# Gate and up of two pairs of steps by seven block products for eight, in four feed-forward stages

## The chip, the cores and the metric

One core of a Trainium2 chip runs the whole program. The metric is the device time in microseconds of one execution. The engines are named TensorE (PE in the profile), VectorE (DVE), ScalarE (ACT), GpSimd (POOL) and SyncE (SP, which issues the loads of the weights).

## The reference

256 tokens of width 1024, in float32, go through a first block (pool mixer, mLSTM, attention, and a feed-forward part with a short convolution) and then through a second block of two layers. Each of these has a feed-forward part, a mixer (NSA attention in the first layer, HGRN2 in the second) and another feed-forward part:

```python
def _swiglu(x, w_gate, w_up, w_down):
    return (jax.nn.silu(x @ w_gate) * (x @ w_up)) @ w_down
x = _layer_norm(alpha * x + 0.5 * _swiglu(x, ffn1_w_gate[i], ffn1_w_up[i], ffn1_w_down[i]), ...)
```

`w_gate` and `w_up` are 1024 x 2816, `w_down` is 2816 x 1024. These four feed-forward parts are what the change is about.

## The kernel before

The plan (from line 438) lists eleven stages: 0, 4 and 8 are linear projections into the mixers, 1, 5 and 9 projections out of them, 2 is the feed-forward part with a convolution, and 3, 6, 7 and 10 are the four plain feed-forward stages.

**Precision.** Every product is made of three matmuls with float32r operands. An operand is split into a high part (ScalarE copies it, which rounds: `act_split` and `act_split_next`, lines 552 and 570) and a low part (VectorE subtracts the high part, `dve_split` and `dve_split_next`, lines 562 and 578). `token_pass` (lines 751 to 753) issues high x high, low x high, high x low, with 128 tokens as the stationary operand and 512 columns of weights moving.

**A step of a feed-forward stage** covers 256 of the 2816 inner columns; there are 11 (`FFN_STEPS`, 0 to 10). For each of the two token tiles `gate_up` (line 911) forms gate and up together, 2 x 256 columns in one PSUM bank: first with the upper 512 rows of the weights (kh = 0, called k0 below), then the lower 512 (k1), 12 matmuls each; 48 a step. ScalarE takes silu of the gate half (line 1003), VectorE multiplies by the up half (line 1055). In the next step TensorE turns the product (four transposes, line 927, into bank 3), ScalarE and VectorE split it into `ghi` (line 1008) and `glo` (line 1060), and `pe_down_step` (line 907) adds its product with two blocks of 128 rows of `w_down` to banks 4 to 7: 24 matmuls. So TensorE's order in a step (`step`, line 934) is k0 of both tiles, the transposes of the step before, k1 of both tiles, the down matmuls of the step before.

**Buffers and queues.** Weights come in halves of 128 x 1024 floats, 512 KB: four of gate and up (two k0, two k1) and two of down a step. SyncE loads them in this order into a ring of six raw slots, each when the low part of the half six places before is made. The split halves go to a ring of six slots (`whi`, `wlo`); ScalarE may overwrite one when TensorE has counted it off in `half_done`. Every engine works through its own order written out by hand (`pe_ffn`, `act_ffn`, `dve_ffn`): for ScalarE ghi, k0 of the next step, silu, silu, k1 and down of the next step; for VectorE glo, the low parts of k0, two products, the low parts of k1 and down. The steps between the first two and the last are a hardware loop (`Fori`) on each of the four engines.

**Around it.** The stage's activations `ahi`, `alo` are made at its opening (`pe_turn`, `act_turned` line 736, `dve_turned` line 741); GpSimd makes a small power for the norms (`pool_rstd`, line 719), loads gain and bias (`pool_load_gb`, lines 633 and 634), and loads the first weights of the NSA stage (`pool_load_nsa`, line 2274) early, while the convolution stage runs. The arena, a large buffer, holds the data of the mixers and lies mostly unused in the feed-forward stages.

Of the kernel before, what the change touches and what calls it, by code (L numbers as in the profile page):

```python
# [63 lines left out]
EXTRA_SLOTS = 2  # L64

# [60 lines left out]
def build_program(nc, io, const_at, out):  # L126
    ctx = ExitStack()
    with ctx:
# [218 lines left out]

        KC_AT = (32, 160, 224, 352)
# [60 lines left out]
        stored = sem("stored")  # L409
        dve_chain = sem("dve_chain")  # L410
# [46 lines left out]
        w_halves, slab0, half0 = [], [0], [0]  # L457

        def add_half(slab, mode, part, extra=None):
            ring = sum(x[3] < HALF_SLOTS for x in w_halves)  # L460
            w_halves.append((slab, mode, part, ring % HALF_SLOTS if extra is None else HALF_SLOTS + extra))

        PROJ_ORDER = {1: (0, 1), 5: (0, 1), 9: (0, 1)}
        for n, e in enumerate(plan):
# [18 lines left out]
            else:  # L483
                for j in range(FFN_STEPS):
                    g = b + (3 * j - 1 if j else 0)
                    for i in range(4):
                        m, x = divmod(i, 2) if e[0] == "conv" and j else (i % 2, i // 2)
                        add_half(g + m, "part", x)
# [17 lines left out]
        for h, (_, mode, part, _) in enumerate(w_halves):  # L506
            if mode != "part" and part == 1:
                landed.append(landed[-1])
                continue
            landings[h % RAW_SLOTS] += 1  # L510
            landed.append((h % RAW_SLOTS, landings[h % RAW_SLOTS]))

        def raw_pair(h):

            at = h % RAW_SLOTS
            return raw[:, at:at + 2, :].rearrange("p s (k n) -> p (s k) n", k=4)

        def raw_half(h):
# [6 lines left out]
            return raw[:, h % RAW_SLOTS, :]  # L525
# [29 lines left out]
        def dve_split(dve, h):  # L555
# [6 lines left out]
            dve.tensor_tensor(lo, raw_half(h), hi.bitcast(F32), ALU.subtract).then_inc(lo_ready, 1)  # L562

# [169 lines left out]

        def act_turned(act, p, a, h):
# [152 lines left out]
        def silu_count(n):  # L887

            return FFN_STEPS + 2 * FFN_STEPS * ffn_index(n)
# [27 lines left out]
        def pe_ffn(pe, n, p):  # L917
            f = ffn_index(n)
            mults, turns = 2 * FFN_STEPS * f, (FFN_STEPS + 1) * f

            def gate_up(h, a, kh):
                return pe_pair(pe, h + 2 * kh, kh, a, ps[:, a, :], kh == 0, kh == 1)

            def turn(tiles):
                for x in range(2):
                    for a in tiles:
                        last = pe.transpose(ps[:, 3, x * T + a * P:x * T + (a + 1) * P],  # L927
                                            gated[:, a, x * P:(x + 1) * P], ident)
                last.then_inc(g_turned, 1)

            for a in range(NT):
                pe_normed(pe, p, half0[n], a, ps[:, a, :], gu_done)

            def step(j, by_mults, by_halves):
                h = body(n, 1)
# [2324 lines left out]
```

## Time and profile before

| | us |
|---|---|
| median of three runs | 1361.31 |
| lowest and highest of them | 1361.13, 1361.77 |
| span of the profiled execution, first to last instruction | 1361.0 |
| TensorE busy | 1349.7 |
| VectorE busy | 883.2 |
| ScalarE busy | 682.4 |
| GpSimd busy | 123.1 |

The profiled execution has its span alone, no device time of its own; the span is 0.3 us below the median of the runs. A feed-forward step lasts 16.8 us, the four stages hold 44 of them, so these are over half of the time. The line numbers of the rows are those of the kernel before. A TensorE row shows an instruction's own duration, which overlaps with the next; how far apart two of them start is read from their start times.

### The profile page before, as it was taken

The numbers are of one execution on the slowest core, as the hardware profiler recorded it, in microseconds if no ns is written. First come the engines' busy times: TensorE is split into PE (matmuls) and PEld (weight loads), VectorE is DVE, ScalarE is ACT, GpSimd is POOL, SyncE is SP. The second block draws the span as 40 slices with busy tenths as digits, with TensorE's granted clock in tenths as the row PEclk, the third lists the DMA queues.
The fourth block names the chain that finished last, engine by engine and source line by source line (L and its number), as shares of the span: only waits on it lengthen the run. The fifth ranks groups of instructions, "written<-read, shape, count | busy, mean of one in ns | idle before, by whom it ended". The sixth has DMA issues, their size and how long they took to land.

```text
span 1361.0 us, 21006 instructions
## 1 busy us (share of the span) xinstructions
PE 1349.7 (99%) x7477; PEld 1158.8 (85%) x7477; DVE 883.2 (65%) x1280; ACT 682.4 (50%) x1037; POOL 123.1 (9%) x235
## 2 busy tenths in 40 slices
PE   9999999999999999999999999999999999999997
PEld 6988999998888889988888888888889988888886
DVE  5877876676555584688655558555576988755555
ACT  6673655554444435595444444444446854444441
POOL 5431000000000011282000000000000001000000
PEclk9999999999999999999999999999999999999999
DMA  9435865564555547504655554655555434655550
GB/s 317 155 99 179 294 196 184 187 191 156 189 189 189 190 136 226 177 2 154 229 189 186 185 195 154 239 185 185 185 159 189 163 108 156 204 190 190 188 186 31
DMA packets 189944, 241.64 MB, mean 178 GB/s; under 512 B 7809, under 2 KB 171922, under 8 KB 189890
## 3 DMA queue, kind: packets, MB, share of 16 engines
q1 hardware_dynamic: 184304, 226.52, 50.9%
q0 software_dynamic: 5296, 13.29, 3.1%
q10 hardware_dynamic: 290, 1.11, 0.2%
q8 instruction: 35, 0.57, 0.2%
q14 instruction: 19, 0.16, 0.0%
HBM read 238.24 MB, written 1.07 MB: 176 GB/s over the span
## 4 chain that ended last, share of the span: by engine, by line
PE 98%; DVE 1%; POOL 1%; DMA 0%; ACT 0%; issue 0%; DVEq 0%; POOLq 0%
PE ps L751 20%; PE ps L753 20%; PE ps L752 20%; PE ps L583 6%; PE ps L585 6%; PE ps L584 6%; PE ps L774 2%; PE ps L775 2%; PE ps L781 2%; PE ps L927 1%; PE ps L1466 1%; PE ps L2756 1%; PE ps L902 1%; PE ps L1477 1%; PE ps L727 1%; PE ps L2338 1%
## 5 line engine op out<-in xcount | busy, mean ns | idle before, releaser
L578 DVE TENSOR_TENSOR wlo<-raw,whi 128x1024 fp32r<-128x1024 f32 x270 | 323.2, 1223 | 121.3 <-ACT whi L570 118.0
L570 ACT ACTIVATE whi<-raw 128x1024 fp32r<-128x1024 f32 x270 | 277.3, 1056 | 117.6 <-PE ps L753 95.2
L751 PE MATMUL ps<-whi,ahi 128*128 128x512 f32 x776 | 308.2, 397 | 0.0
L753 PE MATMUL ps<-wlo,ahi 128*128 128x512 f32 x776 | 302.7, 390 | 0.0
L752 PE MATMUL ps<-whi,alo 128*128 128x512 f32 x776 | 302.4, 390 | 0.0
L562 DVE TENSOR_TENSOR wlo<-raw,whi 128x1024 fp32r<-128x1024 f32 x142 | 168.8, 1221 | 35.4 <-ACT whi L552 35.1
L583 PE MATMUL ps<-ahi,whi 128*128 128x256 f32 x624 | 177.9, 285 | 0.0
L585 PE MATMUL ps<-ahi,wlo 128*128 128x256 f32 x624 | 177.3, 284 | 0.0
L584 PE MATMUL ps<-alo,whi 128*128 128x256 f32 x624 | 177.2, 284 | 0.0
L753 PEld LDWEIGHTS ps<-wlo,ahi 128*128 128x128 f32 x776 | 145.7, 188 | 31.5
L751 PEld LDWEIGHTS ps<-whi,ahi 128*128 128x128 f32 x776 | 145.9, 188 | 30.0 <-issue 0.9
L752 PEld LDWEIGHTS ps<-whi,alo 128*128 128x128 f32 x776 | 146.0, 188 | 29.0 <-issue 0.2
L552 ACT ACTIVATE whi<-raw 128x1024 fp32r<-128x1024 f32 x142 | 144.4, 1054 | 37.6 <-PE ps L753 23.4
L751 PE MATMUL ps<-whi,ghi 128*128 128x512 f32 x400 | 156.5, 391 | 0.0
L752 PE MATMUL ps<-whi,glo 128*128 128x512 f32 x400 | 155.8, 389 | 0.0
L753 PE MATMUL ps<-wlo,ghi 128*128 128x512 f32 x400 | 155.7, 389 | 0.0
L583 PEld LDWEIGHTS ps<-ahi,whi 128*128 128x128 f32 x624 | 120.3, 193 | 0.9 <-issue 0.3
L1060 DVE TENSOR_TENSOR glo<-ps,ghi 128x512 fp32r<-128x512 f32 x40 | 27.7, 692 | 143.8 <-ACT ghi L1008 143.8
L584 PEld LDWEIGHTS ps<-alo,whi 128*128 128x128 f32 x624 | 120.4, 193 | 0.5
L585 PEld LDWEIGHTS ps<-ahi,wlo 128*128 128x128 f32 x624 | 120.4, 193 | 0.0
L1008 ACT ACTIVATE ghi<-ps 128x512 fp32r<-128x512 f32 x40 | 24.0, 600 | 172.6 <-PE ps L927 172.6
L719 POOL TENSOR_TENSOR rstd<-spread_sq,consts 128x1 f32<-128x1 f32 x16 | 12.9, 808 | 975.2 <-DVE spread_sq L686 973.6
(438 smaller groups left out, 1806.5 us busy)
## 6 DMA issues: line engine op xcount, KB each, us to landing
raw<-ffn_w_gate SPq DMA_DIRECT2D x88, 512.0 KB, 3.7
raw<-ffn_w_up SPq DMA_DIRECT2D x88, 512.0 KB, 4.7
raw<-ffn_w_down SPq DMA_DIRECT2D x88, 512.0 KB, 4.3
raw<-w_up SPq DMA_DIRECT2D x44, 512.0 KB, 4.4
raw<-w_down SPq DMA_DIRECT2D x22, 512.0 KB, 4.2
raw<-w_in SPq DMA_DIRECT2D x16, 512.0 KB, 5.3
raw<-nsa_w_in SPq DMA_DIRECT2D x8, 1024.0 KB, 5.1
raw<-hgrn_w_in SPq DMA_DIRECT2D x16, 512.0 KB, 4.7
```

Source lines behind the costliest of these rows:

```text
L552: act.activation(split_half(w_slots(slot)[0], mode), raw_half(h), ACT.Copy).then_inc(hi_ready, 1)
L562: dve.tensor_tensor(lo, raw_half(h), hi.bitcast(F32), ALU.subtract).then_inc(lo_ready, 1)
L570: act.activation(split_half(w_slots(slot)[0], mode), raw_half(h), ACT.Copy).then_inc(hi_ready, 1)
L578: dve.tensor_tensor(lo, raw_half(h), hi.bitcast(F32), ALU.subtract).then_inc(lo_ready, 1)
L583: pe.matmul(dst, wh, ah, start=first, stop=False, skip_group_check=True)
L584: pe.matmul(dst, wh, al, start=False, stop=False, skip_group_check=True)
L585: return pe.matmul(dst, wl, ah, start=False, stop=last, skip_group_check=True)
L751: pe.matmul(dst, a_h, w_h, start=first, stop=False, skip_group_check=True)
L752: pe.matmul(dst, a_l, w_h, start=False, stop=False, skip_group_check=True)
L753: return pe.matmul(dst, a_h, w_l, start=False, stop=last, skip_group_check=True)
L774: pe.matmul(dst, a_h, wh[:, :, k, :], start=first and k == 0, stop=False, skip_group_check=True)
L1060: dve.tensor_tensor(lo[:, :, cols], ps[:, 3, :].rearrange("p (x t) -> p x t", x=2)[:, :, cols], hi[:, :, cols].bitcast(F32), ALU.subtract) ...
```

## The change

In stages 3, 6, 7 and 10 the steps 3 and 4, and the steps 6 and 7, are made as a pair. The pair's gate columns (2 x 256) and up columns are the two block columns, the weights' upper and lower 512 rows the two block rows: blocks b11 (gate, upper), b12 (up, upper), b21, b22 of 512 x 512. With the two token tiles and the two halves of the depth this is a 2 x 2 by 2 x 2 product of blocks, and it is made by seven products of 12 matmuls: b21, b11, b22 with plain or summed activations, t1 to t4 being differences of blocks: t1 = b12 - b11, t2 = b22 - t1, t3 = b22 - b12, t4 = b21 - t2.

- The four raw blocks of a pair, 1 MB each, are loaded whole into the arena (`load_block`), those of the first pair behind the down rows of step 1, those of the second in the single step behind the first pair (step 5), and don't pass through the raw ring. `b1_landed` counts r11 and r12.
- VectorE makes the differences (`dve_t`) in the arena, t1 and t2 for the first pair at the end of step 1, for the second pair in step 5 (t1 ahead of its first `glo`), t3 and t4 in the step ahead of the pair.
- Blocks are split 128 x 2048 at a time into two neighbouring slots of the ring of six (`act_block`, `dve_block`), which so holds three blocks. In the order of a stage, `c` counts blocks; for a pair it is b21, b11, t1, t2, down of the step before, t3, b22, t4, then k0 and k1 of the next step and the pair's two down blocks.
- GpSimd makes the sums of activation blocks at a stage's opening (`pool_sums`); ScalarE and VectorE split them once a stage in step 1 (`s_hi`, `s_lo`, in the arena).
- The products are accumulated in banks z, 1 and r, with copies of two partial sums and additions (`v1`, `v5`, `v_u2`, in `xc`); gate and up then have 512 columns each for a tile.
- Tile 0 of the single steps alternates between banks 0 and 2.
- The hardware loops of the four stages are gone, all steps are written out on every engine.
- The loads of the first NSA weights wait for the last pair of stage 3, the load of `r_gain` for that of stage 7. In the NSA and HGRN stages some semaphores are merged, with the order of the work as it was.

The core of the diff (PE, then ACT, then DVE, POOL and SP; functions that build names and counts are left out):

```diff
+DOUBLES = {3: (3, 6), 6: (3, 6), 7: (3, 6), 10: (3, 6)}
+SUM_BUFFERS = {"b21": "r21", "b11": "r11", "t1": "n1", "t2": "n2", "t3": "r12", "b22": "r22", "t4": "r21"}
...
+        _, s_hi = split_view(0, "s_hi", 4, 4, P)
+        _, s_lo = split_view(2048, "s_lo", 4, 4, P)
...
+        x11, x12, x21, x22 = (blocks["n1"][:, i, :] for i in range(4))
+        s_sum = blocks["n2"]
+        xc_flat = xc.rearrange("p a b -> p (a b)")
+        v1, v_u2, v5, g1 = (xc_flat[:, 512 * i:512 * i + 512] for i in range(4))
...
+        def act_block(act, n, c):
+            name, h = order[n][c]
...
+            if name[0] == "t":
+                act.wait_ge(t_ready, 4 * g.d + int(name[1]))
+            else:
+                landed_at, each = block_landed["r" + name[1:]]
+                act.wait_ge(landed_at, each * (g.d + 1))
+            act.wait_ge(half_done, before_in_slot[h + 1] + 1)
+            act.activation(hi, src, ACT.Copy).then_inc(hi_ready, 2)
+        def dve_block(dve, n, c):
...
+            dve.wait_ge(hi_ready, h + 2)
+            dve.tensor_tensor(lo, src, hi.bitcast(F32), ALU.subtract).then_inc(lo_ready, 2)
...
+        def dve_t(dve, g, i):
...
+            if i == 1:
+                dve.wait_ge(b1_landed, 32 * (g.d + 1))
+                dst, a, b = n1, r12, r11
+            elif i == 2:
+                dve.wait_ge(b22_landed, 16 * (g.d + 1))
+                dve.wait_ge(t_ready, 4 * g.d + 1)
+                dst, a, b = n2, r22, n1
+            elif i == 3:
+                dst, a, b = r12, r22, r12
+            else:
+                dve.wait_ge(b21_landed, 16 * (g.d + 1))
+                dve.wait_ge(t_ready, 4 * g.d + 2)
+                dst, a, b = r21, r21, n2
+            dve.tensor_tensor(dst, a, b, ALU.subtract).then_inc(t_ready, 1)
...
+        def pool_sums(pool, p):
...
+            wait_activations(pool, p)
+            for dst, a, kh in ((x11, 0, 0), (x12, 0, 1), (x21, 1, 0), (x22, 1, 1)):
+                hi, lo = (turned_tile(v, a, kh).bitcast(F32) for v in (ahi, alo))
+                last = pool.tensor_tensor(dst.rearrange("p (c n) -> p c n", c=4), hi, lo, ALU.add)
+            chain(last)
+            pool.tensor_tensor(s_sum[:, 2, :], x11, x21, ALU.subtract)
+            chain(pool.tensor_tensor(s_sum[:, 0, :], x21, x22, ALU.add))
+            chain(pool.tensor_tensor(s_sum[:, 1, :], s_sum[:, 0, :], x11, ALU.subtract))
+            pool.tensor_tensor(s_sum[:, 3, :], x12, s_sum[:, 1, :], ALU.subtract).then_inc(sums_ready, 1)
...
+            def single(i):
+                g, k0, k1 = parts[i], parts[i].at["k0"], parts[i].at["k1"]
+                done = mults + 2 * (i - 1)
+                pe.wait_ge(lo_ready, k0 + 2)
+                if g.first == parts[i - 1].first:
+                    pe.wait_ge(gated_ready, done + 1)
+                gate_up(k0, 0, 0, g.first)
+                pe.wait_ge(gated_ready, done + (1 if parts[i - 1].double else 2))
+                gate_up(k0, 1, 0, 1).then_inc(half_done, 2)
+                pe.wait_ge(gated_ready, done + 2)
+                if parts[i - 1].double:
+                    turn(pair_step(0), range(NT))
+                else:
+                    turn(own, range(NT))
+                pe.wait_ge(lo_ready, k1 + 2)
+                gate_up(k1, 0, 1, g.first).then_inc(gu_done, 1)
+                if parts[i - 1].double:
+                    pe.wait_ge(g_ready, turns + parts[i - 1].steps[0] + 1)
+                    turn(pair_step(1), range(NT))
+                gate_up(k1, 1, 1, 1).then_inc(half_done, 2)
+                for j, source in zip(parts[i - 1].steps, ((ghi, glo), (last_ghi, last_glo))):
+                    down_step(g, j, source)
+            def double(i):
+                g = parts[i]
+                d, z, r, done = g.d, g.first, 2 - g.first, mults + 2 * (i - 1)
+                def product(name, act_k, bank, first, last):
...
+                    pe.wait_ge(lo_ready, h + 2)
+                    for k in range(4):
+                        ins = token_pass(pe, ps[:, bank, :], act_k(k), (wh[:, k, :], wl[:, k, :]), first and k == 0, last and k == 3)
+                    ins.then_inc(half_done, 2)
...
+                pe.wait_ge(gated_ready, done + 1)
+                product("b21", block(0, 1), r, True, True)
+                product("b11", block(0, 0), z, True, True)
+                pe.wait_ge(gated_ready, done + 2)
+                pe.wait_ge(s_lo_ready, f + 1)
+                product("t1", block_sum(1), 1, True, True)
+                turn(own, range(NT))
+                pe.wait_ge(snap_ready, 3 * d + 1)
+                product("t2", block_sum(2), z, False, True)
+                down_step(g, parts[i - 1].steps[0], (ghi, glo))
+                pe.wait_ge(snap_ready, 3 * d + 3)
+                product("t3", block_sum(3), z, False, True)
+                product("b22", block_sum(4), 1, False, True)
+                pe.wait_ge(c_ready, 2 * d + 2)
+                product("t4", block(1, 1), z, False, True)
...
+            def single(i):
+                g, c = parts[i], place_of(n, parts[i].at["k0"])
+                before = parts[i - 1]
+                turned((0, 1), turns + before.steps[0] + 1)
+                act_block(act, n, c + 3)
+                if i == 1:
+                    act.wait_ge(sums_ready, f + 1)
+                    act.wait_ge(half_done, half0[n])
+                    act.activation(s_hi.rearrange("p a k n -> p (a k n)"), s_sum.rearrange("p a n -> p (a n)"),
+                                   ACT.Copy).then_inc(s_hi_ready, 1)
+                if before.double:
+                    turned((0, 1), turns + before.steps[1] + 1, last_ghi)
+                for a in range(NT):
+                    silu(i, a)
+                act_block(act, n, c + 4)
+                act_block(act, n, c + 5)
+                if before.double:
+                    act_block(act, n, c + 6)
+            def double(i):
+                g, c = parts[i], place_of(n, parts[i].at["b21"])
+                d, z = g.d, ps[:, g.first, :]
+                act_block(act, n, c + 3)
+                act.wait_ge(half_done, g.at["b11"] + 2)
+                act.activation(v1, z, ACT.Copy).then_inc(snap_ready, 1)
+                act_block(act, n, c + 4)
+                act.wait_ge(half_done, g.at["t1"] + 2)
+                act.activation(v5, ps[:, 1, :], ACT.Copy).then_inc(snap_ready, 1)
+                turned((0, 1), turns + parts[i - 1].steps[0] + 1)
+                act_block(act, n, c + 5)
+                act.wait_ge(half_done, g.at["t2"] + 2)
+                act.activation(v_u2, z, ACT.Copy).then_inc(snap_ready, 1)
+                act.wait_ge(c_ready, 2 * d + 1)
+                act.activation(v1, v1, ACT.Silu).then_inc(silu_ready, 1)
+                act_block(act, n, c + 6)
+                act_block(act, n, c + 7)
+                act_block(act, n, c + 8)
+                act_block(act, n, c + 9)
+                act.wait_ge(half_done, g.at["t4"] + 2)
+                act.activation(g1, z, ACT.Silu).then_inc(silu_ready, 1)
+                act_block(act, n, c + 10)
...
+            def single(i):
+                g, c = parts[i], place_of(n, parts[i].at["k0"])
+                before, following = parts[i - 1], parts[i + 1]
+                late = following.double and (before.double or i == 1)
+                if late:
+                    dve_t(dve, following, 1)
+                turned((0, 1), turns + before.steps[0] + 1)
+                dve_block(dve, n, c + 3)
+                if before.double:
+                    turned((0, 1), turns + before.steps[1] + 1, last_ghi, last_glo)
+                    c += 1
+                product(i, 0)
+                if late:
+                    dve_t(dve, following, 2)
+                product(i, 1)
+                if i == 1:
+                    dve.wait_ge(s_hi_ready, f + 1)
+                    dve.tensor_tensor(s_lo.rearrange("p a k n -> p (a k n)"), s_sum.rearrange("p a n -> p (a n)"),
+                                      s_hi.rearrange("p a k n -> p (a k n)").bitcast(F32), ALU.subtract).then_inc(s_lo_ready, 1)
+                if before.double:
+                    dve_block(dve, n, c + 3)
+                if following.double:
+                    dve_t(dve, following, 3)
+                dve_block(dve, n, c + 4)
+                if following.double:
+                    dve_t(dve, following, 4)
+                dve_block(dve, n, c + 5)
+                if not following.double and i + 2 < final and parts[i + 2].double:
+                    dve_t(dve, parts[i + 2], 1)
+                    dve_t(dve, parts[i + 2], 2)
+            def double(i):
+                g, c = parts[i], place_of(n, parts[i].at["b21"])
+                d, z, r = g.d, ps[:, g.first, :], ps[:, 2 - g.first, :]
+                dve_block(dve, n, c + 3)
+                dve.wait_ge(snap_ready, 3 * d + 1)
+                dve.tensor_tensor(v1, r, v1, ALU.add).then_inc(c_ready, 1)
+                dve_block(dve, n, c + 4)
+                turned((0, 1), turns + parts[i - 1].steps[0] + 1)
+                dve_block(dve, n, c + 5)
+                dve_block(dve, n, c + 6)
+                dve_block(dve, n, c + 7)
+                dve.wait_ge(half_done, g.at["t3"] + 2)
+                dve.wait_ge(snap_ready, 3 * d + 3)
+                dve.tensor_tensor(v5, z, v5, ALU.add).then_inc(c_ready, 1)
+                dve_block(dve, n, c + 8)
+                dve.wait_ge(half_done, g.at["b22"] + 2)
+                link(dve, dve_chain, "dve", dve.tensor_tensor(v_u2, ps[:, 1, :], v_u2, ALU.add))
+                dve.wait_ge(silu_ready, silus + 2 * i + 1)
+                dve.tensor_tensor(v1, v1, v_u2, ALU.mult).then_inc(gated_ready, 1)
+                dve_block(dve, n, c + 9)
+                dve.wait_ge(silu_ready, silus + 2 * i + 2)
+                dve.wait_ge(c_ready, 2 * d + 2)
+                dve.tensor_tensor(g1, g1, v5, ALU.mult).then_inc(gated_ready, 1)
+                dve_block(dve, n, c + 10)
...
-            pool.wait_ge(a_ready, tile_half(1, 1, 1))
+            pool.wait_ge(half_done, last_double(3).at["t4"] + 2)
...
+            def block_free(n, g, name):
+                before = doubles[g.d - 1] if g.d else None
+                if before is not None and (before in groups[n] or n == 7):
+                    reader = {"r11": "t1", "r12": "t3", "r22": "b22", "r21": "t4"}[name]
+                    sp.wait_ge(lo_ready, before.at[reader] + 2)
+                else:
+                    sp.wait_ge(half_done, half0[2 if n == 3 else n])
+            def load_block(n, g, name, mats):
...
+                block_free(n, g, name)
+                sp.dma_start(blocks[name], mats[int(name[2]) - 1][row:row + 512, col:col + 512]
+                             .rearrange("(k p) n -> p k n", p=P)).then_inc(block_landed[name][0], 16)
+            def load_ffn(n, mats):
...
+                    if not g.double:
...
+                    after_double = len(g.downs) == 2
+                    if after_double and following is not None:
+                        load_block(n, following, "r11", mats)
+                    for x, (j, h) in enumerate(g.downs.items()):
...
+                        if after_double and x == 0 and following is not None:
+                            for name in ("r12", "r22", "r21"):
+                                load_block(n, following, name, mats)
+                    if i == 1 and following is not None:
+                        for name in ("r11", "r12", "r22", "r21"):
+                            load_block(n, following, name, mats)
...
-                if p == 5:
+                if p > 4:
+                    pool_sums(pool, p - 1)
+                if p == 6:
+                    pool.wait_ge(half_done, last_double(7).at["t4"] + 2)
                     pool.dma_start(r_gain, io["hgrn_norm_gain_2"].rearrange("a d -> d a")).then_inc(r_gain_landed, 16)
```

## Rows read from the trace of the kernel before

**Rows 1.** The page: busy time and share of the span; the chain that ended last.
```profile
PE 1349.7 (99%) x7477; PEld 1158.8 (85%) x7477; DVE 883.2 (65%) x1280; ACT 682.4 (50%) x1037; POOL 123.1 (9%) x235
...
PE 98%; DVE 1%; POOL 1%; DMA 0%; ACT 0%; issue 0%; DVEq 0%; POOLq 0%
```

**Rows 2.** The page's costliest groups: name, count, busy us, mean ns, idle before.
```profile
L751 PE MATMUL ps<-whi,ahi 128*128 128x512 f32 x776 | 308.2, 397 | 0.0
L753 PE MATMUL ps<-wlo,ahi 128*128 128x512 f32 x776 | 302.7, 390 | 0.0
```

**Rows 3.** Stretches: length, then PE, PEld, DVE, ACT, POOL busy (instructions), clock, DMA share, GB/s.
```profile
376.00:392.80 16.80, 16.80 (x78) 13.89 (x77) 8.61 (x10) 7.29 (x9) 0.00 (x0) 1.00 0.58 185
...
660.00:677.00 17.00, 17.00 (x78) 14.06 (x78) 12.49 (x13) 9.89 (x12) 0.00 (x0) 1.00 0.88 291
...
309.00:317.00 8.00, 8.00 (x44) 6.71 (x44) 3.83 (x7) 4.27 (x7) 0.00 (x0) 1.00 0.11 40
```

**Rows 4.** Timeline, TensorE, around one step of stage 3: start us, duration us, instruction.
```profile
374.49 0.39 PE L751 MATMUL ps<-whi,ahi 128*128 128x512 f32 x1
...
383.14 0.39 PE L751 MATMUL ps<-whi,ahi 128*128 128x512 f32 x1
...
391.30 0.39 PE L751 MATMUL ps<-whi,ahi 128*128 128x512 f32 x1
...
394.02 0.39 PE L751 MATMUL ps<-whi,ahi 128*128 128x512 f32 x1
```

**Rows 5.** Timeline of the same step, ScalarE and VectorE, idle time before in brackets.
```profile
380.57 0.60 ACT L1008 ACTIVATE ghi<-ps 128x512 fp32r<-128x512 f32 x1 [4.82 <-PE ps L927]
381.06 2.00 ACT L570 ACTIVATE whi<-raw 128x1024 fp32r<-128x1024 f32 x2
381.20 0.69 DVE L1060 TENSOR_TENSOR glo<-ps,ghi 128x512 fp32r<-128x512 f32 x1 [4.19 <-ACT ghi L1008]
382.15 2.36 DVE L578 TENSOR_TENSOR wlo<-raw,whi 128x1024 fp32r<-128x1024 f32 x2 [0.26 <-ACT whi L570]
383.34 0.38 ACT L1003 ACTIVATE ffn_buf<-ps 128x256 f32<-128x256 f32 x1 [0.28 <-PE ps L753]
```

**Rows 6.** Groups by line and shape, VectorE and ScalarE: the widths that the change uses.
```profile
L2961 DVE TENSOR_TENSOR arena<-arena 128x2048 f32<-128x2048 f32 x1 | 2.3, 2292 | 0.0
...
L741 DVE TENSOR_TENSOR alo<-ps,ahi 128x512 fp32r<-128x512 f32 x32 | 21.6, 687 | 12.7 <-ACT ahi L736 12.7
...
L2843 ACT ACTIVATE arena<-arena 128x2048 f32<-128x2048 f32 x1 | 1.9, 1920 | 0.0
...
L1191 ACT ACTIVATE ffn_buf<-ffn_buf 128x512 f32<-128x512 f32 x11 | 7.0, 633 | 26.7 <-DVE ffn_buf L1259 26.7
```

**Rows 7.** Timeline, stage 0: GpSimd's widest operations and VectorE's beside them.
```profile
46.38 2.41 DVE L562 TENSOR_TENSOR wlo<-raw,whi 128x1024 fp32r<-128x1024 f32 x2
47.57 2.16 POOL L2197 TENSOR_TENSOR sq<-sq 128x542 f32<-128x542 f32 x1
...
49.82 1.15 POOL L2198 TENSOR_TENSOR sq<-sq 128x538 f32<-128x538 f32 x1
...
55.73 1.29 POOL L2207 TENSOR_TENSOR xc<-xc,sq 128x512 f32<-128x512 f32 x1
```

**Rows 8.** Timeline, the opening of stage 6 and its step 1.
```profile
646.56 0.69 DVE L660 SCALAR_TENSOR_TENSOR xc<-ps,x_tok 128x512 f32<-128x512 f32 x1
...
654.12 2.35 DVE L562 TENSOR_TENSOR wlo<-raw,whi 128x1024 fp32r<-128x1024 f32 x2
...
655.07 0.53 POOL L634 DMA_DIRECT2D sq<-ln_bias  x1
...
656.39 0.41 DVE L1055 TENSOR_TENSOR ffn_buf<-ffn_buf,ps 128x256 f32<-128x256 f32 x1
...
659.79 4.63 DVE L562 TENSOR_TENSOR wlo<-raw,whi 128x1024 fp32r<-128x1024 f32 x4 [0.53 <-ACT whi L552]
...
664.31 0.60 ACT L1008 ACTIVATE ghi<-ps 128x512 fp32r<-128x512 f32 x1 [1.70 <-PE ps L927]
```

**Rows 9.** The page's DMA issues: KB each, median us from issue to landing.
```profile
raw<-nsa_w_in SPq DMA_DIRECT2D x8, 1024.0 KB, 5.1
...
arena<-nsa_cmp_w POOLq DMA_DIRECT2D x2, 1024.0 KB, 10.9
```

More of the change, by code:

```diff
@@ L885, in ffn_index, with mult_count, single_count @@
             return (3, 6, 7, 10).index(n)
-        def silu_count(n):
-            return FFN_STEPS + 2 * FFN_STEPS * ffn_index(n)
+        def mult_count(n):
+            return 2 * sum(len(groups[m]) for m in groups if m < n)
+        def single_count(n):
+            return sum(not g.double for m in groups if m < n for g in groups[m])
         def pe_down(pe, h, x, a, n, first=False, last=False, gated_parts=(ghi, glo)):
@@ L917, in pe_ffn, with gate_up @@
         def pe_ffn(pe, n, p):
[L918 to L924, printed above, removed]
+            f, parts = ffn_index(n), groups[n]
+            mults, turns = mult_count(n), (FFN_STEPS + 1) * f
+            final = len(parts) - 1
+            def gate_up(h, a, kh, bank):
+                return pe_pair(pe, h, kh, a, ps[:, bank, :], kh == 0, kh == 1)
@@ new lines, in pair_step, with down_step @@
+            def pair_step(i):
+                return lambda a, x: (v1, g1)[a][:, i * 256 + x * P:i * 256 + (x + 1) * P]
+            def down_step(g, j, source):
+                h = g.downs[j]
+                pe.wait_ge(g_ready, turns + j + 1)
+                for x in range(2):
+                    pe.wait_ge(lo_ready, h + x + 1)
+                    for a in range(NT):
+                        for m in range(2):
+                            last = pe_down(pe, h + x, x, a, m, j == 0 and x == 0, gated_parts=source)
+                    last.then_inc(half_done, 1)
@@ L1027, in act_ffn @@
+            act_table(act, ACT.Silu)
+            silu(0, 0)
+            silu(0, 1)
+            act_block(act, n, 3)
+            act_block(act, n, 4)
+            for i in range(1, final):
+                if parts[i].double:
+                    double(i)
+                else:
+                    single(i)
             b = half0[n + 1]
+            act.wait_ge(half_done, last_double(n).at["b22"] + 2)
             act_split(act, b - 2)
@@ L1075, in dve_ffn @@
+            product(0, 0)
+            product(0, 1)
+            dve_block(dve, n, 3)
+            dve_block(dve, n, 4)
+            for i in range(1, final):
+                if parts[i].double:
+                    double(i)
+                else:
+                    single(i)
             b = half0[n + 1]
```

351 lines of the change are left out of this document (214 added, 137 removed).

## The prediction

> **What bounds the kernel now.** I read four views in this order. First the page's busy shares and its chain that ended last [rows 1]: TensorE is busy for 1349.7 of 1361.0 us and holds 98% of the chain, while VectorE is busy 65% and ScalarE 50%. Second the costliest groups [rows 2]: the 128x512 matmuls of lines 751 to 753 are the largest part, and all three have 0.0 idle before them. Third the stretches of one step of a feed-forward stage [rows 3]: 16.80 us, TensorE busy throughout, VectorE 8.6, ScalarE 7.3, at a granted clock of 1.00 (the upper level, 2.4 GHz). Fourth the timeline of such a step [rows 4, 5]. So time is gained only by issuing less on TensorE, and it is lost only where a helper engine is late for it. The question is whether twice the helper work in a pair of steps still hides.
>
> **The price of a matmul.** A row's 390 ns is not it, since matmuls overlap. In [rows 4] twelve of them (line 751 at 391.30, again at 394.02) are 2.72 us apart, 0.227 us each; a step is 72 of them and four transposes, 374.49 to 391.30 = 16.81 us, of which the transposes take 0.45. By a rule of the Trainium skill (TensorE: Matmul & The Clock Gate, Back-to-back issue gap) load-and-multiply pairs of 512 columns sustain about 131 ns; the trace disagrees with its 227. By that figure the saving below would be 12.6 us; the measurement decides.
>
> **What is removed.** A pair of steps needs gate and up of 2 token tiles x 2 halves of the depth: 8 block products of 4 x 3 = 12 matmuls, 96. The scheme has 7, 84. The 48 matmuls of the two down steps and the eight transposes stay. Saved: 12 x 0.227 = 2.72 us a pair, with two pairs in each of four stages 8 x 2.72 = **21.8 us**. Written-out code in place of hardware loops: at a loop's end the trace shows no gap (the period 16.81 spans it), and straight-line stretches show TensorE just as full (the third of [rows 3]); zero either way.
>
> **What is added.** Per pair: VectorE makes 7 low halves of 128x2048 for 8 of 128x1024, four differences t1 to t4, three PSUM additions. [Rows 6] price them: 2.29 us for 2048 columns on VectorE, 1.92 on ScalarE, 0.69 and 0.60 to 0.63 for 512. VectorE goes from 2 x 8.6 = 17.2 to 7 x 2.29 + 4 x 2.29 + 4 x 1.18 + 3 x 0.69 + 2 x 0.69 + 2 x 0.69 = 34.7 us, against 30.9 us of TensorE in the pair; only because the differences are put into the single steps around does it fit. ScalarE: 7 x 1.92 + 4 x 1.0 + 3 x 0.60 + 2 x 0.63 + 2 x 0.60 = 21.7 us. So I laid out a timetable of the double step from these durations and the handoffs of [rows 4, 5]: ScalarE starts 0.20 us after a product's last slot (383.34 against 383.14), VectorE 0.03 us after ScalarE. D = 0 is the first matmul of b21.
> TensorE, if never held: b21 to 2.72, b11 5.44, t1 8.16, transposes 8.61, t2 11.33, down 16.77, t3 19.49, b22 22.21, t4 24.93.
> ScalarE (the ring holds three blocks, so a block's split waits for the product three before): t2 2.9 to 4.8, v1 copy 6.2, down 8.2, v5 copy 9.0, ghi 9.6, t3 11.5, v_u2 copy 12.1, silu 12.8, b22 14.7, t4 17.0 to 18.9 (it waits for the down step's second half), next k0 19.7 to 21.7, next k1 24.4, silu 25.8, down 27.8.
> VectorE: t2 4.9 to 7.2, v1 7.9, down 10.2, glo 10.9, t3 13.8, b22 17.0, t4 18.9 to 21.2, v5 21.9, k0 24.3, v_u2 25.0, product 25.7, k1 28.1, product 28.8, down 31.1.
> Ready against wanted: t2 7.2 / 8.6; glo 10.9 / 11.3; t3 13.8 / 16.8; b22 17.0 / 19.5; t4 with v5 21.9 / 22.2; next k0 24.3 / 24.9; the pair's second product 28.8 / 30.4. Nothing is late, but two margins are 0.3 to 0.4 us: if the cover goes, t4 is late next, and what queues behind it on VectorE is k0. Bounds for what these margins leak: nothing, or (each of the two 0.3 us over its margin) 0.6 us a pair, 5 us in all. I take zero, as every duration in them is a row.
>
> The single step between the two pairs (step 5) is another matter. Its VectorE order is the rest of the pair (free at 31.1 - 24.9 = 6.2 in its own time), then t1 (8.5), then glo (9.2). TensorE wants glo before it may overwrite bank 3 with the second set of transposes, at 5.44 + 0.45 + 2.72 = 8.6. It waits **0.6 us**, once a stage: 2.4 us. Bounds: 0, and 2.3 (the whole of t1) a stage, 9 us; I take the timetable's. Behind t1 on VectorE are glo, the split of the second down step and the products; with them 3 us late nothing of TensorE's is reached. Steps 2 and 8, the other neighbours of a pair, have glo before the differences or none to make, and wait for nothing.
>
> GpSimd makes the sums of the activations, eight operations of 128x512 at 1.15 to 1.29 us [rows 7], 10 us, behind two gain and bias transfers that it issues. In stage 6 these end at 655.6 and ScalarE comes to its wait for the sums at about 667 (ghi at 664.31, 0.6, a pair of splits 2.0) [rows 8]. 655.6 + 10 = 666: just in time. ScalarE late by x delays silu, k1 and the down split; VectorE then has the sums' low half (2.29), t1 and t2 (4.5) ahead of the next glo, which the timetable has ready at 7.9 of the next step against 11.3 wanted. So the first 3 us of lateness cost nothing. Stage 3 has 5 us more, having issued its transfers before.
>
> Transfers: bytes are the same, but four blocks of 1 MB now go ahead of the k0 of step 2. In stage 6 they wait for the projection's last product (read by line 660 at 646.56, [rows 8]); at the 291 GB/s that the queues reached in 660 to 677 [rows 3] 4.2 MB take 14 us, to 661, and k0's 1 MB 3.6 us, to 664.6, where ScalarE asks for it at 664.9. Hidden, barely; lateness would add to the sums' below (A). In stage 3 the queue is idle then (share 0.11 in 309 to 317 [rows 3]). One 1 MB transfer lands in 5.1 us [rows 9]. In the second pair r12, r22, r21 go out as t3, b22, t4 are split (13.8, 17.0, 21.2), and the down rows behind them at 24.3, landing by about 30; ScalarE asks for those at 24.9 + 6.7 = 31.6. The NSA stage's first weights (10.9 us to land, [rows 9]) move from the convolution stage to the end of stage 3's second pair, some 50 us ahead of that stage. GpSimd holds its two memsets and the rstd behind that wait; nothing asks for them earlier. The NSA and HGRN edits rename semaphores: zero. r_gain moves from stage 6 to the last pair of stage 7, still a stage before its reader, and the rstd queued behind its wait is asked for only at that stage's end: zero.
>
> **Sum.** 21.8 - 2.4 = 19.4 us off. The profiled execution spans 1361.0, 0.3 below the median of 1361.3: 1361.3 - 19.4 = **1341.9 us**.
>
> **Rivals.**
> A, the sums are locked out, and thin margins leak (chance 0.20): [rows 7] show a GpSimd operation of 542 columns that starts at 47.57 under two VectorE splits (46.38 to 48.79) and takes 2.16, and its sister of 538 columns, beside operations with other inputs, 1.15. With every one of the eight held for a split of 1.2, the sums end near 675, 8 us late; but VectorE only has six splits there [rows 8], so 5 us is the most: 667 becomes 672. Past the free 3 us it costs TensorE 1 to 2 us in each of stages 6, 7, 10: 3 to 6 us, and up to 5 from the margins. 1345 to 1351. Against: VectorE is idle or reads PSUM from 656.5 to 659.8. The Trainium skill (SBUF — State Buffer, two separate sides) says the pair of ports is an exclusive lock between GpSimd and a VectorE operation with two SBUF inputs; by that rule, the trace agrees, A's lower part is due.
> B, most of the gain is given back (0.05): the handoffs in a pair are slower than in the quiet steps (91% of VectorE's pair is busy: 22.7 of 24.9), t4 and k0 slip 0.7 to 1 us each: 1.4 to 2 us a pair, 11 to 16 us; 1353 to 1358.
> C, the other side (0.05): the split chain paces the pair. From a slot freed to a low half ready is 0.2 + 1.92 + 0.03 + 2.29 = 4.4 us; two products cover 5.4. If, through VectorE's queue order (additions waiting ahead of a split), only one product covers it, TensorE waits 4.4 - 2.7 = 1.7 us at t2, b22, t4 and k0: 6.8 a pair, 54 us, less 21.8: slower by 30 us, 1394. It decides from 2.7 us of waiting a pair. For: VectorE's order in the pair is fixed by hand. Against: the timetable puts every addition at a point where its input is there.
> The rest (0.02) is no change. That the change computes eight products anyway is excluded by its code: seven calls of 12.
>
> **How the numbers follow.** My case has 0.68: from 1339.5 (no wait at all) to 1345. The range must reach into A: 1339 to 1350 holds 0.68 + most of 0.20. From this kernel about 0.2% (2.7 us) can be told from no change. Faster by more: 0.68 + 0.20 + 0.05 less a little = 0.92; within: 0.03; slower: 0.05.
>
> **What the profile should show.** Products of 12 matmuls 2.72 us apart inside a pair; 24.9 us from b21 to the next k0; matmuls fewer by 96; VectorE busy up by 8 x 17.5 = 140 us, ScalarE by 8 x 7 = 56 (and by 9 and 8 for the sums); a wait of TensorE on VectorE's glo of about 0.6 us once a stage, in step 5; none on the splits. The prediction is wrong if TensorE waits on low halves inside the pairs (B, C), or if ScalarE waits long for GpSimd's sums in step 1 and glo of step 2 is late (A).

## The result and the profile after

| | before | changed |
|---|---|---|
| median of 16 runs each, us | 1362.62 | 1359.30 |
| lowest and highest, us | 1361.13, 1365.15 | 1356.80, 1364.24 |
| span of the profiled execution, us | 1361.0 | 1356.6 |

The ratio is 0.9977, with a 95% interval of 0.997 to 0.9985: 3.3 us faster, where 19.4 were forecast. The time lies outside the range given.

The changed kernel's page: busy time and share, then two of the costliest groups (as in [rows 1, 2]). The last line is from the page of the kernel before.
```profile
PE 1335.0 (98%) x7380; PEld 1144.7 (84%) x7381; DVE 1050.8 (77%) x1316; ACT 738.8 (54%) x1041; POOL 178.8 (13%) x267
...
L640 DVE TENSOR_TENSOR wlo<-raw,whi 128x1024 fp32r<-128x1024 f32 x294 | 380.8, 1328 | 65.5 <-ACT whi L630 63.6
...
L899 PE MATMUL ps<-whi,ahi 128*128 128x512 f32 x616 | 248.1, 403 | 10.1 <-DVE wlo L640 10.1
...
L578 DVE TENSOR_TENSOR wlo<-raw,whi 128x1024 fp32r<-128x1024 f32 x270 | 323.2, 1223 | 121.3 <-ACT whi L570 118.0
```
The reader should see three things. TensorE has 97 matmul records fewer (the code issues 96 fewer) and 14.7 us less busy time. VectorE's mean low half of 128x1024 takes 1328 ns where it took 1223. And the matmuls of line 899 have 10.1 us of idle time before them, released by those low halves; before, that column held 0.0.

Where a matmul stood in both traces tells where the time went. The same matmuls are taken in each stage: the first of the opening's high pass, the first with `last_ghi` at the end.

| us between them | before | changed | difference |
|---|---|---|---|
| stage 3, opening to end | 174.85 | 169.43 | -5.42 |
| end of 3 to end of 6 | 334.19 | 334.04 | -0.15 |
| end of 6 to end of 7 | 186.93 | 186.83 | -0.10 |
| end of 7 to end of 10 | 333.18 | 334.17 | +0.99 |

Stage 3 gains all of its 5.44 us. Stages 6 and 7 each lose about as much again as their pairs save, stage 10 a microsecond more. The waits of TensorE, longest first, in the changed kernel (engine, line, for whom: us in total, times, longest) say how:
```profile
PE ps L899 <- DVE wlo L640: 10.1, 3, 3.4
PE ps L1644 <- DVE zeros L1732: 1.2, 1, 1.2
```
The first line is three waits, one in each of those stages. This is the timeline of stage 6's opening there:
```profile
648.98 7.57 DVE L640 TENSOR_TENSOR wlo<-raw,whi 128x1024 fp32r<-128x1024 f32 x2
649.36 0.57 POOL L766 DMA_DIRECT2D sq<-ln_gain  x1 [5.03 <-DVE alo L889]
...
650.48 4.99 POOL L875 TENSOR_TENSOR arena<-ahi,alo 128x512 f32<-128x512 f32 x4
...
655.54 2.16 POOL L877 TENSOR_TENSOR arena<-arena 128x512 f32<-128x512 f32 x1
...
657.14 8.33 DVE L640 TENSOR_TENSOR wlo<-raw,whi 128x1024 fp32r<-128x1024 f32 x4
```
Two low halves, the k0 of step 1, that took 2.35 us at this place before [rows 8] take 7.57: they are not through until GpSimd's four additions (650.48 to 655.47) are. The first half takes its usual 1.22 us, and this is the second alone:
```profile
650.11 6.44 DVE L640 TENSOR_TENSOR wlo<-raw,whi 128x1024 fp32r<-128x1024 f32 x1
```
TensorE wanted it at 653.2. Its own timeline at that point:
```profile
652.18 1.07 PE L929 MATMUL ps<-whi,alo 128*128 128x512 f32 x4
656.61 0.68 PE L899 MATMUL ps<-whi,ahi 128*128 128x512 f32 x1 [3.36 <-DVE wlo L640]
657.08 0.63 PE L900 MATMUL ps<-whi,alo 128*128 128x512 f32 x1
...
659.64 0.63 PE L900 MATMUL ps<-whi,alo 128*128 128x512 f32 x1
660.07 0.45 PE L901 MATMUL ps<-wlo,ahi 128*128 128x512 f32 x1
660.36 0.40 PE L899 MATMUL ps<-whi,ahi 128*128 128x512 f32 x1
```
After an idle time of 3.36 us the matmuls are 0.43 us apart and not 0.227, eight of them here, some 13 in stage 10. Stretches over both places (columns as in [rows 3]) show the granted clock:
```profile
649.00:657.00 8.00, 4.64 (x20) 3.57 (x19) 8.00 (x5) 4.83 (x8) 7.54 (x7) 0.99 1.04 403
657.00:661.00 4.00, 4.00 (x12) 3.13 (x11) 4.00 (x4) 0.45 (x1) 3.92 (x3) 0.60 0.85 254
1177.00:1181.00 4.00, 4.00 (x11) 3.14 (x10) 4.00 (x4) 0.26 (x1) 3.92 (x3) 0.50 0.95 301
```
0.50 is the lower level of 1.2 GHz; the stretch with 0.60 holds its end. So a stage pays 3.5 us for the wait and its edge, and then for the clock: in stage 6 the nine spacings from 656.61 to 660.36 take 3.75 us where nine of 0.227 take 2.04, 1.7 us more; in stage 10, counted in the same way, it is 2.9 us.

**Theories.** L: GpSimd's sums shut VectorE out of its low halves, and that is the whole loss; the pairs give what their matmuls say. L1 adds that the port is held across the four additions because GpSimd waits nowhere between them. W: something else eats the gain, the written-out code or the pairs.

### The profile page after: what moved, and what is told of

It reads as the page before. It is cut to its first block, busy times and chain, and to the rows that moved or that the text cites. A ratio compares the mean times of both kernels' runs of the same rounds, so it can differ in the third digit from the quotient of the medians.

```text
span 1356.6 us, 19292 instructions
## 1 busy us (share of the span) xinstructions
PE 1335.0 (98%) x7380; PEld 1144.7 (84%) x7381; DVE 1050.8 (77%) x1316; ACT 738.8 (54%) x1041; POOL 178.8 (13%) x267
## 4 chain that ended last, share of the span: by engine, by line
PE 96%; DVE 3%; DMA 0%; ACT 0%; POOL 0%; issue 0%; SPq 0%; DVEq 0%
PE ps L899 20%; PE ps L900 20%; PE ps L901 20%; PE ps L716 6%; PE ps L718 6%; PE ps L717 6%; PE ps L922 2%; PE ps L929 2%; PE ps L923 2%; DVE wlo L640 2%; PE ps L1080 1%; PE ps L1775 1%; PE ps L3059 1%; PE ps L1054 1%; PE ps L1786 1%; PE ps L860 1%
## 5 line engine op out<-in xcount | busy, mean ns | idle before, releaser
L640 DVE TENSOR_TENSOR wlo<-raw,whi 128x1024 fp32r<-128x1024 f32 x294 | 380.8, 1328 | 65.5 <-ACT whi L630 63.6
L630 ACT ACTIVATE whi<-raw 128x1024 fp32r<-128x1024 f32 x294 | 298.5, 1053 | 88.5 <-PE ps L901 72.9
L899 PE MATMUL ps<-whi,ahi 128*128 128x512 f32 x616 | 248.1, 403 | 10.1 <-DVE wlo L640 10.1
L900 PE MATMUL ps<-whi,alo 128*128 128x512 f32 x616 | 242.9, 394 | 0.0
L901 PE MATMUL ps<-wlo,ahi 128*128 128x512 f32 x616 | 242.5, 394 | 0.0
L677 DVE TENSOR_TENSOR wlo<-arena,whi 128x2048 fp32r<-128x2048 f32 x56 | 128.4, 2292 | 43.5 <-ACT whi L666 42.8
L899 PEld LDWEIGHTS ps<-whi,ahi 128*128 128x128 f32 x616 | 117.3, 190 | 36.0 <-DVE wlo L640 11.4
L666 ACT ACTIVATE whi<-arena 128x2048 fp32r<-128x2048 f32 x56 | 107.3, 1916 | 67.9 <-PE ps L901 67.9
L901 PEld LDWEIGHTS ps<-wlo,ahi 128*128 128x128 f32 x616 | 117.4, 191 | 25.7
L900 PEld LDWEIGHTS ps<-whi,alo 128*128 128x128 f32 x616 | 117.4, 191 | 23.1 <-issue 0.2
L711 DVE TENSOR_TENSOR wlo<-raw,whi 128x1024 fp32r<-128x1024 f32 x54 | 64.9, 1223 | 36.1 <-ACT whi L703 36.1
L703 ACT ACTIVATE whi<-raw 128x1024 fp32r<-128x1024 f32 x54 | 56.5, 1056 | 41.9 <-PE ps L718 21.8
```

Source lines behind the costliest of these rows:

```text
L630: act.activation(split_half(w_slots(slot)[0], mode), raw_half(h), ACT.Copy).then_inc(hi_ready, 1)
L666: act.activation(hi, src, ACT.Copy).then_inc(hi_ready, 2)
L677: dve.tensor_tensor(lo, src, hi.bitcast(F32), ALU.subtract).then_inc(lo_ready, 2)
L703: act.activation(split_half(w_slots(slot)[0], mode), raw_half(h), ACT.Copy).then_inc(hi_ready, 1)
L899: pe.matmul(dst, a_h, w_h, start=first, stop=False, skip_group_check=True)
L900: pe.matmul(dst, a_l, w_h, start=False, stop=False, skip_group_check=True)
```

## The experiments

The profiled spans carry a scatter that arises ahead of stage 3: its first matmul stands between 310.8 and 314.5 us in the runs. So beside each median stands the profiled time from that matmul to the end of the span; it is 1361.0 - 312.16 = 1048.8 us before, 1356.6 - 312.45 = 1044.2 in the changed kernel.

### The sums on VectorE

```diff
             product(0, 0)
+            dve.wait_ge(a_ready, tile_half(p, 1, 1))
+            dve_sums(dve, 0)
             product(0, 1)
             dve_block(dve, n, 3)
             dve_block(dve, n, 4)
+            dve_sums(dve, 1)
```
`dve_sums` holds the eight operations of `pool_sums`, the four additions in part 0, the rest in part 1; the calls on GpSimd are gone.

> The changed kernel with the eight operations of the activation sums moved from GpSimd to VectorE (four additions behind the first product of step 0, four operations ahead of glo in step 1; 8 x 0.69 = 5.5 us of VectorE a stage). Theory L (GpSimd's sums shut VectorE out of its low halves at the openings of stages 6, 7 and 10, TensorE waits 3.4 us and then runs some 2 us at its lower clock, 5.3 us a stage): the 16 us come back, about 1343 us, no wait of TensorE on a low half, every stage 5.4 us shorter than before. Rival W (the gain is lost to the written-out code or to the pairs themselves): no change, about 1359 us.

Measured: 1340.92 us, ratio 0.9849 (0.9829 to 0.9869), 21.75 us off by the medians; from stage 3 on 1027.4, 21.4 less than before. Taken once more, beside the three runs at the end of this section:

> The kernel with the sums on VectorE once more, beside the three above on the same chip: 1341 us, so that their differences to it can be read.

1342.07 us, ratio 0.9853 (0.9839 to 0.9867), 20.7 us off by the medians, and 1027.5 from stage 3 on. The opening of stage 6 in the timeline of the first of the two:
```profile
647.77 2.35 DVE L640 TENSOR_TENSOR wlo<-raw,whi 128x1024 fp32r<-128x1024 f32 x2
...
650.37 2.49 DVE L875 TENSOR_TENSOR arena<-ahi,alo 128x512 f32<-128x512 f32 x4
652.90 0.42 DVE L1311 TENSOR_TENSOR ffn_buf<-ffn_buf,ps 128x256 f32<-128x256 f32 x1
653.42 4.63 DVE L640 TENSOR_TENSOR wlo<-raw,whi 128x1024 fp32r<-128x1024 f32 x4
...
660.02 0.69 DVE L881 TENSOR_TENSOR arena<-arena 128x512 f32<-128x512 f32 x1
660.63 0.68 DVE L1317 TENSOR_TENSOR glo<-ps,ghi 128x512 fp32r<-128x512 f32 x1
```
The two halves take 2.35 us again, and the same four additions 2.49 us on VectorE where they took 4.99 on GpSimd. No wait of TensorE on a low half is left. Of the 21.8 us that the matmuls promised, 21.4 are there. W falls: with the pairs and the written-out code in place the loss is gone.

### A wait behind each addition

```diff
-                last = pool.tensor_tensor(dst.rearrange("p (c n) -> p c n", c=4), hi, lo, ALU.add)
-            chain(last)
+                chain(pool.tensor_tensor(dst.rearrange("p (c n) -> p c n", c=4), hi, lo, ALU.add))
```

> The changed kernel with a wait of GpSimd on itself behind each of the four additions, where there was one behind the fourth. If VectorE is let in between two GpSimd operations only where GpSimd waits (theory L1), the second low half of the opening is held for one addition of 1.2 us and ends near 653, where TensorE wants it at 653.2 (stage 6): the wait of 3.4 us and the low clock go, about 1343 to 1346 us. If the port is given away after every operation anyway, or not at all until GpSimd is through (L2): as the changed kernel, 1359 us.

Measured: 1344.69 us, ratio 0.9872 (0.9856 to 0.9889); from stage 3 on 1031.2. Stage 6:
```profile
647.83 3.90 DVE L640 TENSOR_TENSOR wlo<-raw,whi 128x1024 fp32r<-128x1024 f32 x2
...
649.32 7.17 POOL L875 TENSOR_TENSOR arena<-ahi,alo 128x512 f32<-128x512 f32 x4
651.65 0.41 DVE L1309 TENSOR_TENSOR ffn_buf<-ffn_buf,ps 128x256 f32<-128x256 f32 x1
652.53 0.42 DVE L1309 TENSOR_TENSOR ffn_buf<-ffn_buf,ps 128x256 f32<-128x256 f32 x1 [0.48 <-ACT ffn_buf L1221]
```
With a wait behind each addition VectorE is let in behind the first: the halves take 3.90 and not 7.57, and now the additions are the ones that are stretched, 7.17 for 4.99. TensorE's wait at the opening is gone; of the 3.8 us left beside the sums on VectorE, 1.8 are three waits at the first pair, as in the next experiment.

So at this place L1's forecast came true. As a rule L1 is too strong, and the changed kernel's own trace shows it. This is the opening of its stage 3, where the additions are the same, unlinked:
```profile
317.93 2.19 POOL L875 TENSOR_TENSOR arena<-ahi,alo 128x512 f32<-128x512 f32 x1 [185.21 <-DVE alo L889]
318.89 2.31 DVE L640 TENSOR_TENSOR wlo<-raw,whi 128x1024 fp32r<-128x1024 f32 x1
...
320.09 2.26 POOL L875 TENSOR_TENSOR arena<-ahi,alo 128x512 f32<-128x512 f32 x1
```
The low half of 318.89 is through at 321.20, after one addition and not after four: the two engines took turns without any wait between the additions. What differs is the order of the starts. In the openings of stages 6, 7 and 10 the second low half begins 0.36 to 0.40 us ahead of the first addition, and is held for the whole run of four. Where a low half begins while a GpSimd operation runs, it is let in behind that one, linked or not; line 877, behind which line 878 follows unlinked, shows it in each stage (657.14: 1.65 us). Why the order matters stays open; no run varied it alone, and in stages 6, 7 and 10 the additions also follow at once on two transfers that GpSimd issues, in stage 3 not.

Beside this, the products of line 1309, one input of which is in PSUM, keep their 0.42 us [rows 8] in the middle of GpSimd's additions; the operations seen held here have both inputs in SBUF.

### The sums begun later

```diff
             wait_activations(pool, p)
+            pool.wait_ge(lo_ready, half0[{2: 3, 4: 6, 5: 7, 7: 10}[p]] + 6)
```

> The changed kernel with GpSimd's sums begun only when the two low halves that TensorE wants first are made (a wait for them ahead of the additions). Theory L: the wait at the opening goes, but the additions then run from about 651.5 to 656.5 and the rest to 666 (stage 6), over the low halves of k1, wanted at 659.1: VectorE makes four halves from 656.5 against alternating GpSimd operations, the second at about 661: a wait of 1 to 2 us a stage in place of 3.4, without a fall of the clock; 1346 to 1350 us. Rival W: 1359 us.

Measured: 1343.72 us, ratio 0.9863 (0.9847 to 0.9880); from stage 3 on 1030.8. That is below the 1346 to 1350 expected: the wait did not move to k1. What is left, 3.3 us against the sums on VectorE, arises later in the stage: the stretched k1 halves (8.40 us for four) and the late sums make VectorE arrive late at the first pair, and TensorE waits there for t1's low half. Each stage from 6 on loses some 1.1 us, of it 0.8 at this wait of 0.6 with its edge (692.0 in stage 6) and 0.3 at the down matmuls of step 2 (680.25), for which VectorE's `glo` is ready at 680.20.
```profile
PE ps L900 <- DVE wlo L677: 1.7, 3, 0.6
...
689.58 4.49 DVE L677 TENSOR_TENSOR wlo<-arena,whi 128x2048 fp32r<-128x2048 f32 x2
```
The first line is of that kernel's waits, the second of its timeline. Here too a half was let in between two unlinked additions:
```profile
653.46 1.70 DVE L640 TENSOR_TENSOR wlo<-raw,whi 128x1024 fp32r<-128x1024 f32 x1 [0.53 <-ACT whi L630]
...
654.03 2.27 POOL L876 TENSOR_TENSOR arena<-ahi,alo 128x512 f32<-128x512 f32 x1
```
It began during the third addition, was through at 655.15, and held the fourth.

### The kernel before, with the sums added

```diff
                     pool_load_gb(pool, p)
+                    pool_sums(pool, p - 1)
...
             pool_load_gb(pool, 8)
+            pool_sums(pool, 7)
```
`pool_sums` is taken over from the changed kernel, with a buffer of its own (not shown).

> The kernel before, with nothing changed but the same eight GpSimd operations added at the openings of stages 6, 7 and 10 (their results are not used). Theory L: the whole loss appears without any pair: 3 x 5.3 = 16 us slower than before, about 1378 us, VectorE's second low half at each opening 6 us long, TensorE waiting 3.4 us and then at half rate for some 2 to 4 us. Rival W: as before, 1362.6 us.

Measured: 1381.24 us, ratio 1.0141 (1.0118 to 1.0163); from stage 3 on 1066.7, 17.9 more than before. Without a pair anywhere, the halves take 7.57 us, TensorE waits 3.8 us three times, and the clock falls. Its waits, then the timeline, then a stretch:
```profile
PE ps L769 <- DVE ffn_buf L1073: 11.4, 3, 3.8
...
652.93 7.57 DVE L562 TENSOR_TENSOR wlo<-raw,whi 128x1024 fp32r<-128x1024 f32 x2
...
654.42 4.99 POOL L745 TENSOR_TENSOR arena<-ahi,alo 128x512 f32<-128x512 f32 x4
...
661.00:665.00 4.00, 4.00 (x11) 3.15 (x12) 4.00 (x4) 0.40 (x1) 3.92 (x3) 0.57 0.68 172
```
The last thing that TensorE waits for is here the product of line 1073 (0.41 us), which stands on VectorE right behind the held low half: in this kernel tile 0 of every step uses the same bank. So the wait is 0.4 us longer. The sums alone cost 17.9 us here; in the changed kernel, 1044.2 - 1027.4 = 16.8. The two agree to 1.1 us, of which the longer waits (11.4 for 10.1) are 1.3.

### One pair a stage

```diff
-DOUBLES = {3: (3, 6), 6: (3, 6), 7: (3, 6), 10: (3, 6)}
+DOUBLES = {3: (3,), 6: (3,), 7: (3,), 10: (3,)}
```
on the kernel with the sums on VectorE.

> The kernel with the sums on VectorE, and only the first pair (steps 3 and 4) of each stage by seven products; steps 6 and 7 are single again. If each pair saves its 12 matmuls whole (2.72 us) and nothing is paid once a stage: half of the 21.8 us, 10.9 us faster than before, 1351.7 us. If a stage pays a fixed part and the second pair is the one that gains, it is off that line by that part (the sums and the load order cost it more than 1 us: above 1353 us).

Measured: 1354.37 us, ratio 0.9934 (0.9920 to 0.9947). By the medians that is 8.4 us off, 2.5 short of 10.9, and above the 1353 that was to mean a fixed part. The profile says otherwise: the time from stage 3 on, 1352.6 - 314.4 = 1038.2, is 10.6 less than before, and the first matmul of stage 3 stands at 314.4 in this trace where it stood at 312.2 before. The line 0, 10.6, 21.4 has no fixed part that can be seen.

### Written out, without pairs

`DOUBLES` with four empty entries, without the sums and their splits, and with the loads of the first NSA weights and of `r_gain` where they were before.

> No pair at all: the four stages written out as single steps, whole products, no activation sums, tile 0 alternating between two banks, the raw ring as before. If written-out code costs and gives nothing: 1362.6 us, as before. If the loops had hidden costs, faster by more than 1 us; if fetching straight code costs TensorE, slower.

Measured: 1362.57 us, ratio 1.0000 (0.9990 to 1.0011); from stage 3 on 1048.7 against 1048.8. Neither loops nor straight code cost TensorE anything.

### One more operation in the pair

```diff
                 dve_block(dve, n, c + 7)
+                n1 = flat_blocks["n1"]
+                link(dve, dve_chain, "dve", dve.tensor_tensor(n1[:, 0:1024], n1[:, 0:1024], n1[:, 1024:2048], ALU.add))
```
on the kernel with the sums on VectorE.

> The kernel with the sums on VectorE, and one more VectorE operation of 128x1024 in each pair (its result is not used), between the low half of t4 and the addition v5: 1.2 us plus a wait of VectorE on itself. By the timetable of the prediction t4 and v5 are ready at 21.9 of the pair and wanted at 22.2: 1.3 us more makes TensorE wait 1.0 us at t4 in every pair, and k0, next on VectorE, moves by as much: 8 us slower than without it, 1349 us. If VectorE's margin in a pair is larger than the timetable says (over 1.3 us), nothing.

Measured: 1350.52 us, ratio 0.9913 (0.9899 to 0.9927), 8.4 us above the 1342.07 of the kernel without the operation; by the profiles from stage 3 on, 1351.5 - 314.5 = 1037.0 against 1027.5, it is 9.5. Its waits:
```profile
PE ps L900 <- DVE xc L1366: 7.2, 8, 0.9
```
Eight waits, one in each pair, at the addition v5, of 0.9 us each, where 1.0 was expected. With the edges of the wait a pair loses 9.5 / 8 = 1.2 us, so nearly all of the operation's 1.25 us is paid. The idle time bears out the margin of 0.3 to 0.1 us; counted by what the pair loses, the margin saves under 0.1.

## Why the prediction was wrong

**The saving: right.** 12 matmuls of 0.227 us in each of eight pairs, 21.8 us; measured 21.4 from stage 3 on, 21.75 and 20.7 by the medians of two runs, once the sums are off GpSimd. Stage 3 shows it in the changed kernel too. The code written out: zero, as said.

**The timetable of the pair: right to 0.2 us.** In the changed kernel b21 of the first pair begins at 357.97. VectorE and TensorE around t4, in its timeline:
```profile
377.08 2.29 DVE L677 TENSOR_TENSOR wlo<-arena,whi 128x2048 fp32r<-128x2048 f32 x1 [1.86 <-ACT whi L666]
...
379.29 0.68 DVE L1363 TENSOR_TENSOR xc<-ps,xc 128x512 f32<-128x512 f32 x1
...
380.22 0.40 PE L899 MATMUL ps<-whi,ahi 128*128 128x512 f32 x1
```
t4's low half is ready at 21.4 of the pair's time (said: 21.2), v5 at 22.0 (21.9), t4 starts at 22.25 (22.2). The margin of 0.3 was real, and nothing leaked. VectorE's busy time rose by 167.6 us, of it 294 x 0.105 = 31 for the held halves; the other 137 stand against 149 forecast (140, and 9 for the sums). ScalarE's rose by 56.4 for 64.

**The wait for glo in step 5: 2.4 us forecast, none on TensorE.** k0 of that step begins at 382.97 (388.41, where its first transposes begin, less 5.44):
```profile
388.63 2.28 DVE L695 TENSOR_TENSOR arena<-arena 128x2048 f32<-128x2048 f32 x1
...
390.83 0.68 DVE L1316 TENSOR_TENSOR glo<-ps,ghi 128x512 fp32r<-128x512 f32 x1
...
391.57 0.42 PEld L1080 LDWEIGHTS ps<-consts,xc 128*128 128x128 f32 x4 [0.22 <-DVE glo L1316]
```
VectorE was free at 5.7 and not 6.2, and glo ready at 8.5 and not 9.2, where TensorE wants it at 8.6. The weight load waits 0.22 us there, in each stage, but TensorE's second set of transposes begins 3.21 us behind the first, as in step 8 (3.22), where nothing is late. Successive operations of VectorE overlap by some 0.05 to 0.08 us (t1 begins at 388.63, glo at 390.83: 2.20 apart for 2.28); the timetable did not count that, and over its row of operations it came to 0.5 us where VectorE is free and 0.7 at glo.

**The sums: this is the step that failed.** The prediction put them on GpSimd's account only: how late they would be for ScalarE, with 3 us free. It held both facts that decide. It saw in [rows 7] a GpSimd operation made longer by VectorE's halves, and it named the rule of an exclusive lock. The Trainium skill (SBUF — State Buffer, two separate sides) says that whoever starts first holds the port pair for the whole instruction, and the other fully blocks. The trace agrees that one blocks the other (6.44 us for 1.22), and not on who wins: at the opening of stage 6 the low half begins at 650.11, 0.36 us ahead of the first addition, and is the one that is held. The prediction drew one side of the rule, GpSimd held by VectorE, and not VectorE held by GpSimd; and it never asked which low half TensorE wants first at an opening. That is k0 of step 1, made at 648.98 to 656.5 under the additions, wanted at 653.2. ScalarE's wait for the sums, which the prediction watched, cost nothing. Rival A so had the cause and the wrong victim, and a price of 3 to 6 us where it was 16.8 (its upper end, 1351, is also 2 us under the sum of its own terms).

**What it cost: two sizes were missing.** The block lasted at these three openings for all four additions, 5 us, and not for one operation's 1.2. And an idle time of 3.4 us on TensorE is followed by matmuls at the lower clock, which adds 1.7 us (stage 6) to 2.9 (stage 10): of the 16.8 us, 10.1 are waits and the other 6.7 the clock and the edges of the waits.

Stage 3 escaped: GpSimd had issued its transfers before and began at 317.93, during the first of the two low halves, so that the second was held for one addition only (through at 321.20), and TensorE wants them there only at 324.3. The transfers, which the prediction called barely hidden, never held TensorE: the queues moved 403 GB/s at the opening of stage 6 (649 to 657), not 291.

B's sum, 1353 to 1358, lies nearest to the time measured, and its cause (late handoffs in the pair) did not occur. That the kernel came out faster at all, as forecast with 0.92, is the rest of a saving that was right over a loss of three quarters of it that was not seen; it does not speak for the prediction.

## What to carry to other kernels

Work moved to an idle engine is not free if it shares a port with a busy one: list the operations of the other engine that have both inputs in SBUF during those microseconds, and ask which of them the bounding engine wants first. A VectorE operation begun just ahead of a row of unlinked GpSimd operations was kept out for the whole row, 5 us; with a wait behind each of them, or begun while one of them ran, it was held for one. A hand-made timetable from measured durations was good to 0.2 us inside a pair, where the engines did not share anything, and had operations 0.5 to 0.7 us too late at the end of a long row whose overlap it left out; where it says a margin of 0.3 us, an operation of 1.25 us added there costs 1.2.

## What the runs showed of the hardware

- VectorE's subtraction of 128x1024 with both inputs in SBUF is held by GpSimd's operations, 7.57 us for two beside four unlinked additions, 3.90 beside four linked ones, 2.35 alone. With one input in PSUM (128x256, 0.42 us) it is not.
- A low half begun 0.36 to 0.40 us ahead of the first of four unlinked additions was held for all four (6.44 to 6.47 us, six openings in two kernels). One begun during a GpSimd operation was let in behind it, also where the next operation was unlinked (2.31 us at 318.89; 1.70 us at 653.46 with the sums begun later).
- Beside a row of VectorE's low halves the two engines take turns: GpSimd's 128x512 takes 2.15 to 2.29 us and not 1.25, and a low half 2.3 and not 1.22.
- The same addition of 128x512 takes 1.25 us on GpSimd (4.99 for four) and 0.62 to 0.69 on VectorE.
- After TensorE's idle 3.4 us, 8 to 13 matmuls ran 0.43 us apart, at a granted clock of 0.50 (1177 to 1181); waits of 0.9 us, eight times, left the clock at its upper level (mean 0.999).
